# Two-block decoder in split fp32r products: the cross attentions' first key block moved ahead, filler products, gates and small stages reordered

## The reference

```python
for i in range(4):
    kind = i % 3                       # diff attention, hgrn2, chunked sgu, diff attention
    x = x + mix(rmsnorm(x, norm_mix[i]))
    x = x + mem_cross_attention(rmsnorm(x, norm_cross[i]), mem_n, ca_w_q[i], ca_w_kv[i], ca_w_o[i])
    x = x + swiglu(rmsnorm(x, norm_ffn[i]), ffn_w_gu[i], ffn_w_down[i])

def mem_cross_attention(h, mem_n, w_q, w_kv, w_o):
    q = (h @ w_q).reshape(B, S, 4, 256)
    k, v = jnp.split(mem_n @ w_kv, 2, axis=-1)     # keys and values depend on mem alone
    ...
```

## Time and profile before

| | us |
|---|---|
| median of 3 runs | 2652.77 (2650.37 to 2653.67) |
| the profiled execution's own time | 2648.42 |
| its span, first to last instruction | 2646.6 |
| PE busy | 2539.2 (96%) |
| DVE busy | 1312.9 (50%) |
| ACT busy | 1069.2 (40%) |
| mean granted TensorE clock, share of full | 0.988 |

### The profile page before, as it was taken

The page is one execution under the profiler, slowest core; times in us unless marked ns, Lnnn a source line. Parts: engine busy times, 40 slices in busy tenths (PEclk is TensorE's granted clock), DMA queues, the critical chain, the costliest instruction groups (busy, mean ns, idle before and its releaser), DMA issues.

```text
span 2646.6 us, 34129 instructions
## 1 busy us (share of the span) xinstructions
PE 2539.2 (96%) x12082; PEld 1883.7 (71%) x12082; DVE 1312.9 (50%) x1928; ACT 1069.2 (40%) x1633; POOL 55.6 (2%) x86
## 2 busy tenths in 40 slices
PE   8999998899998999999999899999999999999998
PEld 6875442585432678888779787887787887788886
DVE  5644111553212575555556555555656555665554
ACT  4443110451111454444454344445454444554443
POOL 0000000000000000000000000000000000000000
PEclk9999999999999999999999999999999999999999
DMA  7548999548999426365442154554545554253652
GB/s 246 178 160 331 381 409 409 202 154 336 406 409 386 152 96 199 117 216 184 149 165 90 38 194 156 187 189 165 177 153 182 190 190 151 96 181 120 224 190 95
DMA packets 149970, 546.16 MB, mean 206 GB/s; under 512 B 17031, under 2 KB 17232, under 8 KB 149720
## 3 DMA queue, kind: packets, MB, share of 16 engines
q1 hardware_dynamic: 144664, 526.04, 55.6%
q0 software_dynamic: 4912, 17.43, 2.1%
q10 hardware_dynamic: 272, 1.05, 0.1%
HBM read 543.39 MB, written 2.63 MB: 206 GB/s over the span
## 4 chain that ended last, share of the span: by engine, by line
PE 82%; DVE 7%; DMA 5%; ACT 3%; issue 2%; POOL 1%; SPq 0%; POOLq 0%; ACTq 0%; DVEq 0%
PE bank L1965 20%; PE bank L1967 19%; PE bank L1966 19%; PE bank L2240 7%; PE bank L2268 3%; DMA stage_w<-in_wide 2%; PE bank L2043 2%; DVE low_w L1107 2%; DMA pair_w<-in_wide 1%; DMA pair_d<-in_down 1%; PE bank L2585 1%; PE bank L2601 1%; PE bank L2534 1%; ACT tmp L944 1%; PE bank L2504 1%
## 5 line engine op out<-in xcount | busy, mean ns | idle before, releaser
L1965 PE MATMUL bank<-high_w,xh 128*128 128x512 f32 x2112 | 844.5, 400 | 30.8 <-DVE xl L1122 13.3
L1107 DVE TENSOR_TENSOR low_w<-stage_w,high_w 128x1024 fp32r<-128x1024 f32 x528 | 641.5, 1223 | 415.5 <-ACT high_w L695 389.1
L1967 PE MATMUL bank<-high_w,xl 128*128 128x512 f32 x2112 | 828.1, 392 | 0.0
L1966 PE MATMUL bank<-low_w,xh 128*128 128x512 f32 x2112 | 826.8, 391 | 0.0
L695 ACT ACTIVATE high_w<-stage_w 128x1024 fp32r<-128x1024 f32 x528 | 554.8, 1059 | 213.6 <-PE bank L1967 183.7
L1965 PEld LDWEIGHTS bank<-high_w,xh 128*128 128x128 f32 x2112 | 399.1, 189 | 126.6 <-issue 33.6
L1967 PEld LDWEIGHTS bank<-high_w,xl 128*128 128x128 f32 x2112 | 398.9, 189 | 85.3
L1966 PEld LDWEIGHTS bank<-low_w,xh 128*128 128x128 f32 x2112 | 399.7, 189 | 78.3
L1465 DVE TENSOR_TENSOR qk<-qk,bank 128x256 f32<-128x256 f32 x32 | 13.5, 421 | 224.9 <-ACT qk L833 224.9
L1965 PE MATMUL bank<-high_d,hidden_h 128*128 128x512 f32 x320 | 124.9, 390 | 0.0
L1967 PE MATMUL bank<-high_d,hidden_l 128*128 128x512 f32 x320 | 124.6, 389 | 0.0
(11 more groups left out here) (294 smaller groups left out, 2800.3 us busy)
## 6 DMA issues: line engine op xcount, KB each, us to landing
stage_w<-in_wide SPq DMA_DIRECT2D x592, 512.0 KB, 4.4
pair_w<-in_wide SPq DMA_DIRECT2D x128, 512.0 KB, 13.4
stage_d<-in_down SPq DMA_DIRECT2D x120, 512.0 KB, 4.4
proj<-in_wide SPq DMA_DIRECT2D x64, 512.0 KB, 13.2
pair_d<-in_down SPq DMA_DIRECT2D x64, 512.0 KB, 14.7
proj<-in_down SPq DMA_DIRECT2D x32, 512.0 KB, 14.7
gain<-in_gains POOLq DMA_DIRECT2D x19, 512.0 KB, 4.6
skew<-bias_dram POOLq DMA_DIRECT2D x1, 1536.0 KB, 15.4
```

The source lines that it names most:

```text
L1107: vec.tensor_tensor(low_w[:, w], stage_w[:, w], high_w[:, w].bitcast(F32), ALU.subtract)\
L1965: pe.matmul(o, hi, wh, start=start, stop=False)
L1966: pe.matmul(o, hi, wl, start=False, stop=False)
L1967: return pe.matmul(o, lo, wh, start=False, stop=stop)
```

## The change

- `plan()` gets `first_keys`: in decoder layers 1, 2 and 3 the first of the cross attention's two key blocks is done ahead, into `keys_ahead` (words of `pair_d[0]`, shared with `high_d`). In layers 2 and 3 it stands between the ffn before and the turn of the mixer's norm, which thereby becomes an early turn inside it; in layer 1 between `hgrn` and the turn of y. The cross attention then has one key block, and the turn of k reads its first half from `keys_ahead`. SP's source index gets a `shift`, since the weights keep their order in memory; the number of transfers is the same.
- In `turn_stage` the `keep_clock(7, 7)` behind hgrn goes, and `keep_clock(7, 2)` behind the ffn stays only where the turn follows the prenorm directly (decoder layer 1, after layer 0's ffn).
- Fillers are added: `keep_clock(0, 3)` in `hgrn` ahead of the state products, and in both expert stages `keep_clock(3, 1)` ahead of `last_down` and `keep_clock(6, 2)` ahead of the last scatter.
- `gates` moves behind one more block and the turn of q, on every engine, and its first two passes become one pass of 128 x 1024 (`1 - lb`) and one of 256 x 1024.
- `lower_bound` moves from behind mem's norm to behind the turn of it.
- Retention's output block waits for its input bank by bank.

```diff
+AHEAD = (1, 2, 3)
...
+    def first_keys(width, blocks):
+        add("linear", what=dict(blocks=1, width=width, chunk=KC, ahead=True, shift=blocks), wide=1, out=1)
+        moved[0] = -1
...
         prenorm()
+        if layer in AHEAD and layer != 1:
+            first_keys(2048 if layer == 2 else 3072, 6 if layer == 2 else 8)
         turn("norm", "s", hook=True)
...
             linear(2, 4096, col=1024, func="sigmoid")
-            add("gates", mixed=1)
             linear(1, 4096, col=2048)
             turn("q", "p")
+            add("gates", mixed=1)
             linear(1, 4096, col=2560)
             turn("gates", "p", chunk=KC)
             linear(2, 4096, col=3072, func="silu")
             add("hgrn", mixed=2)
+            if layer in AHEAD:
+                first_keys(4096, 2)
             turn("y", "s", hook=True)
...
         residual()
         prenorm()
-        linear(2, 3072, col=1024, chunk=KC)
+        moved[0] = 0
+        if layer in AHEAD:
+            linear(1, 3072, col=1024 + WIDE, chunk=KC)
+        else:
+            linear(2, 3072, col=1024, chunk=KC)
         turn("norm", "s", hook=True)
...
+        keys_ahead = pair_d[0][:, 0:T * WIDE].rearrange("p (t n) -> p t n", t=T)
+        def rows_of(s):
+            return keys_ahead if s.ahead else pv(s.width)
...
-                    src = dram["wide"][bass.ds(n + MOE_UNITS * moes, 1), p, :, :].rearrange("a p n -> p (a n)")
+                    at = n + (MOE_UNITS * moes + (shift_of(n) if shift is None else shift))
+                    src = dram["wide"][bass.ds(at, 1), p, :, :].rearrange("a p n -> p (a n)")
...
+                    if of_memory(s):
+                        act.wait_ge(lb_exp, 1)
+                        act.activation(stat[:, 128:160], stat[:, 128:160], ACT.Exp).then_inc(lb_exp, 1)
...
-                    dve.wait_ge(taken[t], s.out)
-                link(vec.tensor_tensor(tv, f, lb, ALU.mult))
-                link(vec.tensor_tensor(f, f, tv, ALU.subtract))
+                    dve.wait_ge(taken[t], s.out - 1)
+                rest = tmp[:, 0:D]
+                link(vec.tensor_scalar(rest, table[:, 0:D], -1.0, 1.0, ALU.mult, ALU.add))
+                link(vec.tensor_tensor(f, f, rest.rearrange("p (t n) -> p t n", t=1).broadcast_to([P, T, D]), ALU.mult))
                 link(vec.tensor_tensor(f, f, lb, ALU.add))
...
-                    elif PLAN[PLAN.index(s) - 1].kind == "hgrn":
-                        keep_clock(7, 7)
-                    turn(s.turn, src, 0, ready(0))
+                    turn(s.turn, src, 0, ready(0), left)
...
                 turn_hidden(STEPS - 1)
+                keep_clock(3, 1)
                 last_down(STEPS - 1)
+                keep_clock(6, 2)
                 scatter(PAIRS - 1, STEPS)
...
-                if s.moe is None and after(s).kind == "prenorm":
+                if s.moe is None and after(s).kind == "prenorm" and after(after(s)).early:
                     keep_clock(7, 2)
                     turn_early(after(s))
...
+                def keep(b):
+                    pe.wait_ge(kept_h, kept(s.turn) + b + 1)
+                    pe.wait_ge(kept_l, kept(s.turn) + b + 1)
+                def second_tile():
+                    keep(2)
+                    turn_heads(1)
                 turn_heads(0)
-                wait_kept(s.turn)
-                pending[1, 0] = lambda: turn_heads(1)
+                pending[0, 0] = lambda: keep(0)
+                pending[0, WP // 2] = lambda: keep(1)
+                pending[1, 0] = second_tile
+                pending[1, WP // 2] = lambda: keep(3)
...
+                pe.wait_ge(hg_decay, 4 * HG_LEVELS + 1)
+                keep_clock(0, 3)
                 pe.wait_ge(hg_x, HG_LEVELS + 1)
```

More of the change, by code:

```diff
@@ L96, in __init__ @@
                  last=False, func="", fused=False, hook=False, early=False, n_heads=0, comps=1, chunks=1, dv=0, causal=False, scale=1.0, which="", layer=0,
-                 by_half=False):
+                 by_half=False, ahead=False, shift=0):
         self.kind = kind
+        self.ahead, self.shift = ahead, shift
         self.wide, self.out, self.down, self.turn, self.norm, self.h, self.soft, self.heads, self.mixed = (
@@ L113, in plan @@
     c = dict.fromkeys(COUNTED, 0)
-    stages = []
+    stages, moved = [], [0]
     def add(kind, turns="", what=(), **counted):
-        stages.append(Stage(kind, c, **dict(what)))
+        stages.append(Stage(kind, c, **{"shift": moved[0], **dict(what)}))
         for k, v in counted.items():
@@ L232 @@
 PLAN, TOTAL = plan()
+AHEAD_OF = {s.turn: s.kind == "turn" and s.src == "k" and PLAN[i - 3].kind == "linear" and PLAN[i - 3].blocks == 1
+            for i, s in enumerate(PLAN) if s.kind == "turn"}
 def kept(m):
@@ L275, in after, with shift_of, of_memory @@
     return PLAN[PLAN.index(s) + 1]
+def shift_of(n):
+    return [p.shift for p in PLAN if p.wide <= n and p.kind in ("linear", "residual", "attention", "gated")][-1]
+def of_memory(s):
+    return PLAN[PLAN.index(s) - 2].src == "mem"
 def lam_init(layer):
@@ L495, in _, with load_wide @@
         def _(sp):
-            def load_wide(n, first=False, moes=0, behind=None):
+            def load_wide(n, first=False, moes=0, behind=None, shift=None):
                 for p in range(WP):
@@ L564, in _ @@
                     moes = moes_ahead(s.wide)
-                    if blocks == 1:
+                    if blocks == 2:
                         load_wide(s.wide + 1, moes=moes)
-                    else:
-                        with sp.Fori(1, blocks + 1) as i:
-                            load_wide(s.wide + i, moes=moes)
+                    elif blocks > 2:
+                        with sp.Fori(1, blocks) as i:
+                            load_wide(s.wide + i, moes=moes, shift=s.shift)
+                    load_wide(s.wide + blocks, moes=moes)
                 elif s.kind == "gated" and s.moe is not None:
@@ L1906, in _ @@
                         last_low(s)
-                    if s.src == "mem":
-                        lower_bound()
                 elif s.kind == "turn":
@@ L1917, in _ @@
                         keep_plain(s.turn, s.chunk, s.scale)
+                    if of_memory(s):
+                        lower_bound()
                     if s.turn == 0:
@@ L2032, in _, with turn @@
             pending = {}
-            def turn(m, src, t, ready=None):
+            def turn(m, src, t, ready=None, left=None):
                 if ready is not None:
@@ L2042, in turn @@
                     for k in range(4):
+                        rows = src if i or left is None else left
                         mm = pe.transpose(bank[2 * t + i][:, k * P:(k + 1) * P],
-                                          src[:, t, (4 * i + k) * P:(4 * i + k + 1) * P], ident[:, :])
+                                          rows[:, t, (4 * i + k) * P:(4 * i + k + 1) * P], ident[:, :])
                     mm.then_inc(turned, 1)
             def outs_of(s, col):
-                p = [p for p in PLAN[:PLAN.index(s)] if p.kind == "linear" and p.col <= col < p.col + p.blocks * WIDE][-1]
-                return p.out + (col + D - p.col) // WIDE
+                p = [p for p in PLAN[:PLAN.index(s)] if p.kind == "linear" and not p.ahead
+                     and p.col <= col + WIDE < p.col + p.blocks * WIDE][-1]
+                return p.out + min((col + D - p.col) // WIDE, p.blocks)
             def turn_stage(s, inside=False):
@@ L2063, in turn_stage @@
                     pv(width)[:, :, 1024:2048] if s.src[0] == "k" else yv
+                left = keys_ahead if s.src == "k" and AHEAD_OF[s.turn] else None
                 if not s.early:
@@ L2087, in turn_stage @@
                         keep_clock(7, 4)
-                    turn(s.turn, src, 1, ready(1))
+                    turn(s.turn, src, 1, ready(1), left)
             def turn_early(s):
```

9 lines of the change are left out of this document (3 added, 6 removed).

## The result

The changed kernel takes 2627.41 us, median of 4 runs (2622.74 to 2631.71), against 2653.22 for the kernel before on the same chip (2650.37 to 2654.09): ratio 0.9912, 95% interval 0.9895 to 0.9928. The forecast was 2628.5. The profiled execution took 2622.74 us with a span of 2620.9, 25.7 less than the span before; the sum had said 24.2.

What follows compares the result with a forecast made beforehand. The prediction took TensorE, busy 96% of the span, to bound the kernel. Its terms, 1.6 + 3.7 + 4.25 + 7.5 + 7.2 + 0 = 24.2 us, came off the 2652.8 median: 2628.5 us, range 2622 to 2638.

Steps and rivals of the forecast that it cites:

- Retention: Retention's output block: PE starts once the first low part is there, not all four; gain 1.6 us.
- Lower bounds: Behind mem's norm: moving lower_bound saves 2.0 us of wait and 1.7 of slow clock; gain 3.7 us.
- Gates: Layer 1's gates: PE works through another block beside them; gain 4.25 us, 2.55 of wait and 1.7 of clock.
- Fillers in hgrn: Ahead of hgrn's state products: output products at full clock, PE gains 2.5 us, the heads' norm about 2.0.
- Keys ahead in hgrn: Block moved behind hgrn: 10.9 us removed later, output block starts 3.4 later; net gain 7.5 us.
- Layers 2 and 3: Keys block between ffn and mixer: fills the boundary's wait, gain 3.6 us each, 7.2 for both.
- Expert stages: New fillers ahead of last_down and last scatter: taken as 0; bounds a loss of 0.8 and a gain of 4.5 us.
- the moved blocks only move the wait: Rival, chance 0.10: in layers 2 and 3 the stall comes back, the 7.2 us are gone: 2635.7 us.
- the clock is not held: Rival, chance 0.22: hgrn's outputs stay slow (2.2), the wait behind the gates lowers the clock (1.7): 2632.5 us.
- the fillers do more: Rival, chance 0.13: old fillers of both expert stages run at full clock, 4.5 us less: 2624 us.
- the slower case: Rival, chance 0.05: idle ahead of hgrn's output block drops the clock, which stays at 1.2 GHz; with 100 us, 2678.

Runs made afterwards that it cites:

- run 6: Changed kernel with retention's four-bank wait and the lower bounds' old place put back: 2630.35 us.
- run 5: Changed kernel with the gates back in front of the block and the turn of q, keeping the new passes: 2626.77 us.
- run 3: Changed kernel without the three filler products ahead of hgrn's state products: 2629.78 us.
- run 12: The version of run 9 without the filler products ahead of hgrn's state products: 2623.60 us against 2619.62.
- run 8: Changed kernel with y's first tile copied out ahead of the last weight parts (ACT and DVE) in layer 1's moved block: 2622.28 us.
- run 4: Changed kernel without the new fillers ahead of last_down and the last scatter in both expert stages: 2625.88 us.
- run 9: Changed kernel with the gates' logarithm later on ACT, y's first parts earlier, and fewer fillers behind the first expert stage: 2619.62 us.
- run 11: Kernel before with only the three filler products ahead of hgrn's state products added: 2647.32 us against 2648.82.
- run 10: The changed kernel measured once more, with no edit: 2626.51 us.

## Why the prediction was right, point by point

- **Retention**: forecast 1.6, measured 1.63, and undone by itself 1.64 (run 6). The start behind it moved along; the first expert stage then took 1.3 longer, with one slow stretch more.
- **Lower bounds**: forecast 2.0 + 1.7, measured 2.14 + 1.63. Run 6 shows both parts going together.
- **Gates**: forecast 4.25, measured 3.97; the wait left is 1.87 where 1.5 was forecast. From the logarithm's end to PE it was 2.74 (1377.87 to 1380.61) for 2.83, but the logarithm itself ended 0.4 later than worked out. What the prediction had not split: 1.6 of it are the shorter passes and 2.4 the move (run 5).
- **Fillers in hgrn**: forecast 2.5 on PE and 2.0 for the heads; measured 2.4 for the outputs and 2.7 for the heads, since the state products, which the sum left out, became 0.4 shorter too. The size was right against a trace in which the outputs were slow, but it isn't a fixed price (runs 3 and 12).
- **Keys ahead in hgrn**: forecast 7.5, measured 8.5. The output block starts 2.5 later than before instead of 3.4, since the heads were 0.7 earlier than forecast. The wait of 4 us is there (3.91), and the slow output block too. This was the step with a rule behind it: the Trainium skill, page "TensorE: Matmul & The Clock Gate", section "Architectural detail: the array is 16× 32×32, not 1× 128×128", has ACT and DVE strictly first in, first out. The trace agrees: y's low part starts at 1487.04, 2.5 us after ACT's `xh` began at 1484.52, behind a copy and a low part that nobody waited for as urgently; with the order changed (run 8) it follows 0.63 behind. ACT's fourth high part ahead of `xh`, 0.6 of the wait, the sum had not listed.
- **Layers 2 and 3**: forecast 3.6 each, measured 3.58 and 3.6.
- **Expert stages**: forecast 0, measured 3.3 in this trace. The term that missed is "I take 0": the old fillers ran at full clock in the second stage (9.55 us for 12.47), and the stage's end came out 2.94 shorter. It was inside the stated bounds (4.5), and over the traces it comes in 3 of 11, so that it is no sure part of the gain: run 4 shows none in the median.
- **The rivals**: that the moved blocks only move the wait is excluded in layers 2 and 3. That the clock is not held did not come true at either of its two places: hgrn's outputs ran at full clock, and the wait of 1.87 behind the gates lowered no clock in eight traces. Its reason, that 2.5 to 4 us of idle stood ahead of each slow stretch, was misread: in the trace before, one stretch starts at 2273.86 behind an idle time of 1.32 us and two more, at 270.24 and 649.12, with PE busy throughout. That the fillers do more came true in the second expert stage of this trace, where it was balanced by the 2.9 lost at the start. Nothing came near the slower case: the longest slow stretch ahead of PE's last product lasted 10.2 us in the 14 traces.

That the median fell within 1.1 us of the forecast owes something to chance: in the profiled execution 28.3 of gains met 2.6 of losses that belong to no edit, and in the second measurement the two medians are 22.3 apart instead of 25.8. The waits that the edits took away are the sure part; the clock part is what one trace before happened to lose.

## What to carry to other kernels

Before a block of work is moved into a gap, write out the in-order queues of the helper engines behind it: the gap came back here at 3.9 us, 2.5 of it because a copy and splits stood ahead of the one operand that TensorE needed, and swapping them was worth as much as some of the change's own edits. Ask of every operation ahead of the critical one who reads its result and when; the logarithm had two blocks of time. And price a filler by several traces, since the slow stretch that it prevents doesn't come in every one.

## What the runs showed of the hardware

- The clock behind a wait of PE, over the 14 traces (both kernels and the 12 runs), from the start of the last product ahead of it to the next one's. At the places that the edits touch: behind 0.7 us (mem) and 1.2 us (retention) it was never slow, 11 of 11 each; behind 1.45 (runs 8, 9, 12) never, 3 of 3; behind 1.87 (gates) never, 8 of 8. Behind 2.6 to 2.9 it was slow in 6 of 7 (mem three times, retention twice in three, run 5's gates), behind 4.2 (gates of the kernel before and run 11) in 2 of 2, behind 3.9 (output block) in 7 of 8, the exception being run 5 with 3.98 us for its 18 products. Such a stretch costs 1 to 2.8 us.
- That table is no rule for short waits. Other places, which no edit touches, have slow stretches that come and go, and they too stand directly behind a wait: at about 2265 (and once at 941), behind 1.7 us, in 6 cases of 28; at about 1870, behind 2.05, in 3 of 14; at 215, behind 2.0 to 3.3, in 7 of 14 (of the changed kernel's two traces, in run 10's alone). So 1.7 us can be followed by half clock, and 1.87 us behind the gates was not in eight traces: the length of the wait alone doesn't decide it. Near 270 and 650 all 14 traces have a slow stretch with no wait ahead. The case at 2273.84 in the kernel before, and its window:

```profile
2273.84 0.79 PE L1965 MATMUL bank<-high_w,xh 128*128 128x512 f32 x1 [1.32 <-ACT proj L968]
```

```profile
2273.84:2277.27 3.43, 3.43 (x8) 2.76 (x9) 3.21 (x11) 1.58 (x4) 0.00 (x0) 0.50 0.09 12
```

- With the transfers at 38 us these stretches make a good part of the 9 us by which runs of one kernel differ. Windows of two traces of the changed kernel, run 10's and the first one's, each from the last product ahead of the wait:

```profile
39.41:49.50 10.09, 8.61 (x36) 6.27 (x35) 5.04 (x5) 4.38 (x5) 0.00 (x0) 1.00 0.70 243
```

```profile
37.91:48.00 10.09, 7.09 (x18) 4.88 (x17) 5.41 (x5) 4.23 (x4) 0.00 (x0) 0.66 0.56 192
```

The second did half the products in 10.09 us. Why the transfer was late there stays open.
- From the scatter's last product to the first filler PE takes 2.35 to 4.6 us, most of it idle without a releaser, and not the same in two traces of one kernel (2.97 and 3.69 for the first stage of the changed one). The program has the end of a branch there, but the trace has no row for it and no run took the wait away; so its cause is only argued.
